# The last down-projection block in seven products, with its operands formed while the block before it is multiplied

## The chip, the cores and the metric

One core of a Trainium2 chip runs the whole kernel as one program. The metric is the device time of one launch in microseconds (us). The engines are TensorE (PE), VectorE (DVE), ScalarE (ACT), GpSimd (POOL) and SyncE (SP), which issues the DMAs. Each has its own instruction queue, worked through in order; they meet only at semaphores. An instruction that waits holds up all that stands behind it on its engine.

## What is computed

Two residual layers run over 768 tokens (512 and 256) of width 1024: a token mixer (mLSTM in layer 0, gated linear attention in layer 1), then a SwiGLU channel mixer. The change touches the channel mixer alone:

```python
D_FF = 2816
def _swiglu(h, w_gu, w_down):
    g, u = jnp.split(h @ w_gu, 2, axis=-1)
    return (jax.nn.silu(g) * u) @ w_down
# in each layer:
h = _rmsnorm(x, norm_ffn_g[i])
x = x + _swiglu(h, ffn_w_gu[i], ffn_w_down[i])
```

## The kernel before

**Splitting into two parts.** Every float32 operand `v` is held as a rounded high part `hi` and the rest `lo = v - hi`. ScalarE writes the high part (a CAST), VectorE the low part (a subtraction). A product is then three matmuls of 128x128 weights on 384 tokens: hi·hi, hi·lo, lo·hi. Tokens are worked on in two halves of 384 (`HT`), and activations lie transposed, channels on partitions.

**Tiles and blocks.** Weights come in tiles of 256 output columns. The 2816 inner channels are eleven groups of 256; group 0 is block 0, groups 2b-1 and 2b are block b, for b = 1 to 5. A "gate" or "up" tile multiplies the 1024 channels of h (eight chunks of 128) into one group. A "down" tile (b, m) multiplies the four chunks of block b into output columns 256m to 256m+255, and adds them to the residual `xT`.

**Seven products.** Plainly, a tile is four groups (two column halves by two token halves); a down tile so done is 4 x 4 chunks x 3 = 48 matmuls (`tile_seq`). The function `fast_tile` does it instead by Winograd's form of Strassen's scheme: a 2x2 block product in seven block products, not eight. A fast down tile is 7 x 2 x 3 = 42 matmuls, a fast gate or up tile 7 x 4 x 3 = 84. For that, sums of blocks are needed on both sides:

- of the weights, four a tile (`fast_sums` and the fourth in `fast_low`): into `s_tmp0`, `s_tmp1` and in place into `raw`. They run on VectorE. The fast tile then has seven weight units, j = 0 to 6, and `fast_high` (ScalarE) and `fast_low` (VectorE) split each in two.
- of the activations, four a block, `T1` to `T4`, besides the plain blocks `B11`, `B21`, `B22`. For h they are made once a layer. For a down block they are made from `sg` and `at` (the silu(gate)·up results of the two groups) while the gate tile after the block runs (`opens`, `middle`), and are stored in `ax0` to `ax5` and `y_parts`.

**Buffers and order.** A weight unit j of the next tile may be split only when product j of the tile at work is done, so while TensorE does tile t, ScalarE and VectorE do the units of tile t+1 between the copies and adds that take tile t out of PSUM. In ScalarE's `fast_work` a tile's four copies out of PSUM (`p1`, `u1`, `p5`, `u2`) stand between the splits; the split of unit 2 waits for the third weight sum, and `p5` stands behind it. Product 5 of a tile waits for the copy `p5` of the same tile. The table `FT` (`fast_order`) sets the order of tiles: gate and up of groups 1 and 2; then for b = 1 to 4 gate and up of group 2b+1, the four down tiles of block b, gate and up of group 2b+2. SyncE loads each tile's weights about two tiles ahead (`load_w`).

**Block 5** is not in `FT`. Its four down tiles follow as plain tiles (`PLAST`): ScalarE and VectorE split whole tiles (`split`, 128x1024), and `last_pair_parts` and `last_parts` split the activations. Under these tiles ScalarE squares each new residual (`squares`), and GpSimd adds the squares into `sq_sum`, one 128x384 add after the other. In layer 0 TensorE needs that sum of the first token half after the third group of the last tile (`first_sum`) for the next norm; in layer 1 right after the last tile (`token_sums`), for the final norm.

## Time and profile before

| what | us |
|---|---|
| median of 3 runs | 1755.4 (1754.39 to 1755.97) |
| the profiled execution | 1752.71 |
| its span, first to last instruction | 1750.9 |
| TensorE busy (matmuls) | 1711.0, 98% |
| VectorE busy | 1164.7, 67% |
| ScalarE busy | 833.5, 48% |
| GpSimd busy | 229.7, 13% |
| mean granted TensorE clock, of full speed | 0.997 |

A line of a timeline gives the start of an instruction (or of a run of like ones, xN) in us from the span's start, its length, the engine, the line of the kernel, the operation with the tile written, the tiles read and the shape, and in brackets the engine's idle time before it with what ended it. Nearly all matmuls have one line, 482, since a helper issues them: they are told apart by their operands. An operation's length is longer than the step to the next one where two overlap in the engine's pipeline; steps are read from starts. The part of the profile that answers the change is the channel mixer's, 376 to 882 us in layer 0 and 1232 to 1738 us in layer 1.

### The profile page before, as it was taken

Reading aid. Unit: us, or ns where it says so; the run is one execution under the profiler, and the core shown is the slowest. Engines: PE = TensorE matmul, PEld = TensorE weight load, DVE = VectorE, ACT = ScalarE, POOL = GpSimd, SP = SyncE. Lnnn points to the kernel's source line nnn. Section 1 sums busy time; section 2 is a strip of 40 time slices with the busy share of each in tenths; the row PEclk is TensorE's granted clock in tenths of the full one; section 3 lists DMA queues with packets and bytes.
Section 4 is the critical chain, followed back from the end, with each engine's and each line's share of the span. In section 5 each row is a group of like instructions: output and inputs, shape, how many; then the busy total and the mean of one; then the engine's idle time right before and its main releaser. Section 6 shows DMA issues by size and latency. Waiting matters only on the chain.

```text
span 1750.9 us, 26390 instructions
## 1 busy us (share of the span) xinstructions
PE 1711.0 (98%) x10042; PEld 1668.6 (95%) x10042; DVE 1164.7 (67%) x2122; ACT 833.5 (48%) x1574; POOL 229.7 (13%) x253
## 2 busy tenths in 40 slices
PE   7999999999999999999999999999999999999998
PEld 6999888999999999999989999999999999999988
DVE  6142455458789898988461366632888888888865
ACT  5222455234455555555442346741445555555543
POOL 4000021360000000000230014425200000000003
PEclk9999999999999999999999999999999999999999
DMA  5320001501313131312232100041031222212121
GB/s 171 121 73 25 25 25 49 166 18 61 97 37 109 37 103 43 98 48 80 82 121 73 49 25 25 25 168 49 19 103 61 65 81 62 84 61 85 61 72 73
DMA packets 108940, 123.75 MB, mean 71 GB/s; under 512 B 4720, under 2 KB 105136, under 8 KB 108560
## 3 DMA queue, kind: packets, MB, share of 16 engines
q1 hardware_dynamic: 107760, 122.00, 21.3%
q8 instruction: 81, 1.33, 0.3%
q14 instruction: 43, 0.35, 0.1%
q10 hardware_dynamic: 1056, 0.07, 0.0%
HBM read 112.62 MB, written 9.44 MB: 70 GB/s over the span
## 4 chain that ended last, share of the span: by engine, by line
PE 80%; DVE 14%; ACT 2%; issue 2%; DMA 1%; POOL 0%; SPq 0%; DVEq 0%; ACTq 0%; POOLq 0%
PE bank L482 79%; DVE xT L1773 4%; DVE w_lo L1731 3%; DVE raw L1715 1%; DVE s_tmp L1718 1%; DVE qkv L1932 1%; DVE s_tmp L1712 1%; DVE w_lo L1689 1%; DVE xT L1950 1%; ACT w_hi L1116 1%; DMA raw<-in_mlstm_w_out_dram 0%; ACT u_five L1214 0%; DVE raw L1736 0%; DVE w_lo L1695 0%; DMA xs<-in_x_prompt_dram 0%
## 5 line engine op out<-in xcount | busy, mean ns | idle before, releaser
L482 PE MATMUL bank<-y_parts,w_hi 128*128 128x384 f32 x1920 | 497.6, 340 | 11.5 <-DVE w_lo L1689 10.4
L482 PE MATMUL bank<-h_hi,w_hi 128*128 128x384 f32 x1280 | 438.6, 343 | 4.5 <-DVE w_lo L1695 1.8
L482 PE MATMUL bank<-h_lo,w_hi 128*128 128x384 f32 x1280 | 432.2, 338 | 0.0
L482 PE MATMUL bank<-h_hi,w_lo 128*128 128x384 f32 x1280 | 431.9, 337 | 0.0
L482 PEld LDWEIGHTS bank<-y_parts,w_hi 128*128 128x128 f32 x1920 | 349.0, 189 | 15.9 <-DVE w_lo L1689 11.6
L482 PE MATMUL bank<-y_parts,w_lo 128*128 128x384 f32 x960 | 324.6, 338 | 0.0
L1158 ACT CAST w_hi<-raw 128x512 fp32r<-128x512 f32 (+1 forms) x360 | 188.9, 526 | 137.9 <-PE bank L482 137.6
L482 PEld LDWEIGHTS bank<-h_hi,w_hi 128*128 128x128 f32 x1280 | 240.6, 188 | 14.5 <-POOL h_lo L2480 3.5
L1731 DVE TENSOR_TENSOR w_lo<-raw,w_hi 128x512 fp32r<-128x512 f32 (+1 forms) x360 | 200.9, 567 | 63.0 <-ACT w_hi L1158 62.0
L482 PEld LDWEIGHTS bank<-h_lo,w_hi 128*128 128x128 f32 x1280 | 240.7, 188 | 1.2 <-issue 0.2
L482 PEld LDWEIGHTS bank<-h_hi,w_lo 128*128 128x128 f32 x1280 | 240.6, 188 | 0.6
L482 PEld LDWEIGHTS bank<-y_parts,w_lo 128*128 128x128 f32 x960 | 181.5, 189 | 0.0
L1689 DVE TENSOR_TENSOR w_lo<-raw,w_hi 128x2048 fp32r<-128x2048 f32 (+2 forms) x40 | 73.0, 1826 | 116.4 <-ACT w_hi L1116 116.2
L482 PE MATMUL bank<-ax,w_hi 128*128 128x384 f32 x512 | 131.4, 338 | 1.1
L1950 DVE TENSOR_TENSOR xT<-xT,bank 128x384 f32<-128x384 f32 x96 | 52.9, 551 | 86.1 <-PE bank L482 82.3
L482 PE MATMUL bank<-w_hi,h_lo 128*128 128x256 f32 x384 | 107.3, 279 | 0.0
L482 PE MATMUL bank<-w_lo,h_hi 128*128 128x256 f32 x384 | 107.3, 279 | 0.0
L482 PE MATMUL bank<-w_hi,h_hi 128*128 128x256 f32 x384 | 107.2, 279 | 0.0
L1116 ACT CAST w_hi<-raw 128x2048 fp32r<-128x2048 f32 (+2 forms) x43 | 64.7, 1506 | 74.8 <-PE bank L482 61.8
L2504 POOL TENSOR_TENSOR sq_sum<-sq_sum,sg 128x384 f32<-128x384 f32 x26 | 27.5, 1058 | 520.8 <-ACT sg L1316 516.7
L482 PEld LDWEIGHTS bank<-ax,w_hi 128*128 128x128 f32 x512 | 92.1, 188 | 3.7 <-ACT u_five L1214 3.7
L1731 DVE TENSOR_TENSOR w_lo<-s_tmp,w_hi 128x512 fp32r<-128x512 f32 (+1 forms) x144 | 81.6, 567 | 7.6 <-ACT w_hi L1158 7.3
(264 smaller groups left out, 2660.7 us busy)
## 6 DMA issues: line engine op xcount, KB each, us to landing
raw<-in_ffn_w_gu_dram SPq DMA_DIRECT2D x44, 1024.0 KB, 5.1
raw<-in_ffn_w_down_dram SPq DMA_DIRECT2D x40, 512.0 KB, 3.5
raw<-in_gla_w_in_dram SPq DMA_DIRECT2D x12, 1024.0 KB, 5.4
raw<-in_mlstm_w_in_dram SPq DMA_DIRECT2D x11, 1024.0 KB, 5.3
x_keep<-xT SPq DMA_DIRECT2D x2, 3072.0 KB, 10.7
xT<-x_keep SPq DMA_DIRECT2D x8, 768.0 KB, 6.6
raw<-in_mlstm_w_out_dram SPq DMA_DIRECT2D x4, 1024.0 KB, 7.1
raw<-in_gla_w_out_dram SPq DMA_DIRECT2D x4, 1024.0 KB, 6.2
```

The source lines that it names most:

```text
L482: return nc.tensor.matmul(out, lhsT, rhs, start=start, stop=stop, skip_group_check=chained)
L1116: nc.scalar.copy(w_hi[s][:, 0:nb, :], raw[s][:, 0:nb, :]).then_inc(w_hi_ready, 1)
L1158: nc.scalar.copy(unit(w_hi, j, nk), w_source(s, j, nk)).then_inc(op_hi if j < 6 else w_hi_ready, 1)
L1689: V.tensor_tensor(w_lo[s][:, 0:nb, :], raw[s][:, 0:nb, :], w_hi[s][:, 0:nb, :].bitcast(F32), ALU.subtract).then_inc(w_lo_ready, 1)
L1712: V.tensor_tensor(s_tmp0[:, 0:nk, :], w_block(s, 0, 0, nk), w_block(s, 1, 0, nk), ALU.subtract).then_inc(op_sum, 1)
L1715: V.tensor_tensor(w_block(s, 1, 0, nk), w_block(s, 1, 0, nk), w_block(s, 1, 1, nk), ALU.add).then_inc(op_sum, 1)
L1718: V.tensor_tensor(s_tmp1[:, 0:nk, :], w_block(s, 1, 0, nk), w_block(s, 0, 0, nk), ALU.subtract).then_inc(op_sum, 1)
L1731: V.tensor_tensor(unit(w_lo, j, nk), w_source(s, j, nk), unit(w_hi, j, nk).bitcast(F32), ALU.subtract).then_inc(op_lo if j < 6 else w_lo_r ...
L1773: return V.tensor_tensor(out, out, src, ALU.add)
L1932: V.scalar_tensor_tensor(out=h_chunk(c, half), in0=xT[:, c, halves[half]], scalar=gain[e][:, c:c + 1], in1=rstd[:, half, :], op0=ALU.mult, ...
L1950: V.tensor_tensor(x, x, src, ALU.add).then_inc(taken[s], 1)
L2504: G.tensor_tensor(sq_sum[:, g // 2, :], sq_sum[:, g // 2, :], sg[:, n % 4, :], ALU.add).then_inc(sq_acc, 1)
```

## The change

Three of the four plain tiles of block 5 become fast tiles. The order of tiles becomes: as before up to block 3, then gate and up of groups 9 and 10, the four down tiles of block 4, three fast down tiles of block 5, and last one plain tile (column block 3), whose weights no longer go through the slot buffers but are split into `y_parts` (`last_w`).

The eight operands of block 5 (`B12` is an eighth, for the plain tile) are formed during the four down tiles of block 4, two a tile (`LATE`). They are stored where h was (`h_hi`, `h_lo`) and in free rows of `y_parts`. ScalarE and VectorE split them (`late_high`, `late_low`), and GpSimd forms the four sums (`late_sums`). GpSimd also forms the four weight sums of every down tile (`down_sums`), 19 a layer; those of gate and up tiles stay on VectorE. The squares of the residual are moved between the last fast tiles, in pieces.

```diff
 def fast_order():
-    for b in range(1, BLOCKS - 1):
+    for b in range(1, BLOCKS - 2):
         out += [("gate", 2 * b + 1, 0), ("up", 2 * b + 1, 0)] + [("down", b, m) for m in range(4)]
         out += [("gate", 2 * b + 2, 0), ("up", 2 * b + 2, 0)]
+    for i in (GROUPS - 2, GROUPS - 1):
+        out += [("gate", i, 0), ("up", i, 0)]
+    out += [("down", BLOCKS - 2, m) for m in range(4)] + [("down", BLOCKS - 1, m) for m in range(3)]
...
+LATE = ((B11, B12), (T1, B21), (T2, T3), (T4, B22))
...
@@ TensorE, after the fast tiles @@
-                q = q0 + PLAST
-                tile_seq(q, 0, a_of(BLOCKS - 1), 4, (a_last_before(0), None, a_last_before(1), None))
-                tile_seq(q, 1, a_of(BLOCKS - 1), 4)
-                tile_seq(q + 1, 0, a_of(BLOCKS - 1), 4)
...
+                tile_begin(q0 + PLAST + 1, 1)
+                pe.wait_ge(a_ready, 4 + 5 * (L + 1))
+                for g in range(4):
...
@@ ScalarE, fast_work @@
+                if late:
+                    late_high(L, late[0])
                 if t >= 2:
                     act.wait_ge(c_out, 3 * (u - 2) + 3)
                 act.wait_ge(p_done, 6 * u + 3)
                 nc.scalar.copy(u_slot(u, "u1"), a).then_inc(p_copied, 1)
...
+                else:
+                    act.wait_ge(raw_loaded[1], 16 * (q + 1))
+                    for k in range(2):
+                        nc.scalar.copy(last_w[0][:, 2 * k:2 * k + 2, :], raw[1][:, 2 * k:2 * k + 2, :]
...
+                if kind == "down" and i == BLOCKS - 1 and m:
+                    squares(PAIRS * L + PLAST, 2 * L + 2, range(4 * m - 4, 4 * m))
...
@@ VectorE, fast_work @@
-                if more:
+                if more and FT[t + 1][0] != "down":
                     fast_sums(L, t + 1)
...
@@ GpSimd @@
+            def down_sums(L, t):
+                pool.wait_ge(raw_loaded[s], 16 * (q + 1))
+                if u:
+                    pool.wait_ge(op_lo, 6 * u - 1)
+                G.tensor_tensor(s_tmp0[:, 0:nk, :], w_block(s, 0, 0, nk), w_block(s, 1, 0, nk), ALU.subtract
...
+                pool.wait_ge(op_sum, 4 * u + 3)
+                pool.wait_ge(op_lo, 6 * u + 1)
+                G.tensor_tensor(w_block(s, 0, 0, nk), w_block(s, 0, 1, nk), s_tmp1[:, 0:nk, :], ALU.subtract
...
+            def ffn(L):
+                for t, (kind, i, m) in enumerate(FT):
+                    if t + 1 < NF and FT[t + 1][0] == "down":
+                        down_sums(L, t + 1)
+                    if kind == "down" and i == BLOCKS - 2:
+                        late_sums(L, m)
...
+                    if kind == "down" and i == BLOCKS - 1 and m:
+                        squares(PAIRS * L + PLAST, 2 * L + 2, range(4 * m - 4, 4 * m))
+                squares(PAIRS * L + PLAST, 2 * L + 2, range(8, 15))
```

GpSimd's queue, before, between the norm's low parts (`h_lo`) and the first squares of layer 0's end; nothing else stands in the whole channel mixer:

```order
L2480 TENSOR_TENSOR h_lo<-qkv,h_hi 128x384 [waits hi_ready] x8
L2587 MEMSET g_hi 128x1024 [waits p_done]
L2588 MEMSET g_lo 128x1024
L2589 MEMSET w_a2_raw 96x1024
L2504 TENSOR_TENSOR sq_sum<-sq_sum,sg 128x384 [waits group_sq,sq_acc,taken0] x2
```

GpSimd's queue after the change, during the first two down tiles of block 4: four weight sums for the second tile, the first sum of block 5's activations, four weight sums for the third tile, two more activation sums:

```order
L2537 TENSOR_TENSOR s_tmp0<-raw1 128x256 [waits op_lo,raw_loaded1]
L2540 TENSOR_TENSOR raw1<-raw1 128x2x128 [waits op_sum]
L2543 TENSOR_TENSOR s_tmp1<-raw1 128x256 [waits op_sum]
L2547 TENSOR_TENSOR raw1<-raw1,s_tmp1 128x2x128 [waits op_lo,op_sum]
L2557 TENSOR_TENSOR sg<-sg 128x768 [waits a_ready,au_lo]
L2537 TENSOR_TENSOR s_tmp0<-raw0 128x256 [waits op_lo,raw_loaded0]
L2540 TENSOR_TENSOR raw0<-raw0 128x2x128 [waits op_sum]
L2543 TENSOR_TENSOR s_tmp1<-raw0 128x256 [waits op_sum]
L2547 TENSOR_TENSOR raw0<-raw0,s_tmp1 128x2x128 [waits op_lo,op_sum]
L2560 TENSOR_TENSOR sg<-at,sg 128x768 [waits au_lo]
L2562 TENSOR_TENSOR sg<-at,sg 128x768 [waits a_ready]
```

A queue that was empty between the norm and the layer's end now runs through all down tiles, each row waiting for VectorE (`op_lo`, `au_lo`).

GpSimd's queue after the change, at the end of layer 0: the weight sums of the last fast tile and then all thirteen adds of squares:

```order
L2547 TENSOR_TENSOR raw0<-raw0,s_tmp1 128x2x128 [waits op_lo,op_sum]
L2527 TENSOR_TENSOR sq_sum<-sq_sum,sg 128x384 [waits group_sq,sq_acc,taken0] x2
L2527 TENSOR_TENSOR sq_sum<-sq_sum,sg 128x384 [waits sq_acc,group_sq,taken1] x4
L2527 TENSOR_TENSOR sq_sum<-sq_sum,sg 128x384 [waits sq_acc,group_sq,taken0] x4
L2527 TENSOR_TENSOR sq_sum<-sq_sum,sg 128x384 [waits sq_acc,group_sq,taken1] x3
```

The adds themselves are the same and in the same order; what moved is the ScalarE squares that they wait for, of which those of the second tile (x4, `taken1`) now stand behind the copies of the last fast tile:

```order
L1248 COPY u_five<-bank2 128x384 [waits p_done,c_out]
L1260 COPY rstd<-bank0 128x384 [waits p_done]
L1342 ACTIVATE sg<-xT 128x384 [waits taken1]
L1342 ACTIVATE sg<-xT 128x384 [waits sq_acc,taken1] x3
```

There ScalarE does its last two copies out of PSUM for the third block-5 tile first, and then the four squares of the second.

## Rows read from the trace of the kernel before

**Rows 1.** the page: busy time, share and instructions of each engine

```profile
PE 1711.0 (98%) x10042; PEld 1668.6 (95%) x10042; DVE 1164.7 (67%) x2122; ACT 833.5 (48%) x1574; POOL 229.7 (13%) x253
```

**Rows 2.** timeline of TensorE, both layers: start, length, line, operation [idle before]

```profile
846.00 1.01 PE L482 MATMUL bank<-y_parts,w_hi 128*128 128x384 f32 x2 [3.57 <-DVE w_lo L1689]
...
1701.75 0.78 PE L482 MATMUL bank<-y_parts,w_hi 128*128 128x384 f32 x2 [3.58 <-DVE w_lo L1689]
```

**Rows 3.** two-microsecond windows: length, busy time of five engines, granted clock, DMA share

```profile
850.00:852.00 2.00, 2.00 (x8) 2.00 (x7) 0.55 (x1) 0.52 (x1) 0.00 (x0) 0.50 0.89 283
1702.00:1704.00 2.00, 2.00 (x8) 2.00 (x8) 2.00 (x4) 0.00 (x0) 0.00 (x0) 0.51 0.53 160
```

**Rows 4.** timeline of VectorE: residual adds of the first plain tile

```profile
850.37 0.55 DVE L1950 TENSOR_TENSOR xT<-xT,bank 128x384 f32<-128x384 f32 x1 [1.42 <-PE bank L482]
853.34 0.55 DVE L1950 TENSOR_TENSOR xT<-xT,bank 128x384 f32<-128x384 f32 x1 [2.42 <-PE bank L482]
...
1705.90 0.56 DVE L1950 TENSOR_TENSOR xT<-xT,bank 128x384 f32<-128x384 f32 x1 [1.19 <-PE bank L482]
```

**Rows 5.** timeline of TensorE: starts of two down tiles, then the fourth tile

```profile
790.67 0.51 PE L482 MATMUL bank<-ax,w_hi 128*128 128x384 f32 x2
...
797.97 0.51 PE L482 MATMUL bank<-ax,w_hi 128*128 128x384 f32 x2
...
810.32 0.34 PE L482 MATMUL bank<-y_parts,w_lo 128*128 128x384 f32 x1
810.79 0.61 PE L482 MATMUL bank<-ax,w_hi 128*128 128x384 f32 x2
```

**Rows 6.** timeline of ScalarE: in the third and fourth down tile of block four

```profile
799.26 0.48 ACT L1185 COPY u_tmp<-bank 128x384 f32<-128x384 f32 x1 [0.69 <-PE bank L482]
...
802.40 0.48 ACT L1214 COPY u_five<-bank 128x384 f32<-128x384 f32 x1 [0.26 <-PE bank L482]
...
809.74 0.62 ACT L1158 CAST w_hi<-s_tmp 128x512 fp32r<-128x512 f32 x1 [0.60 <-DVE s_tmp L1718]
810.27 0.47 ACT L1214 COPY u_five<-bank 128x384 f32<-128x384 f32 x1
```

**Rows 7.** timeline of VectorE: third down tile of block four

```profile
800.00 0.42 DVE L1712 TENSOR_TENSOR s_tmp<-raw 128x256 f32<-128x256 f32 x1
...
802.84 0.55 DVE L1773 TENSOR_TENSOR xT<-xT,bank 128x384 f32<-128x384 f32 x1
803.32 0.42 DVE L1731 TENSOR_TENSOR w_lo<-s_tmp,w_hi 128x256 fp32r<-128x256 f32 x1
803.65 0.42 DVE L1731 TENSOR_TENSOR w_lo<-raw,w_hi 128x256 fp32r<-128x256 f32 x1
```

**Rows 8.** groups of VectorE by form: busy, mean ns, idle before

```profile
L1749 DVE TENSOR_TENSOR ax<-sg,ax 128x768 fp32r<-128x768 f32 x16 | 15.2, 951 | 0.0
```

**Rows 9.** timelines of GpSimd and VectorE, one window each

```profile
344.45 2.74 POOL L2473 TENSOR_TENSOR sq_new<-xT 128x384 f32<-128x384 f32 x1
...
344.21 2.29 DVE L1689 TENSOR_TENSOR w_lo<-raw,w_hi 128x2048 fp32r<-128x2048 f32 x1
...
375.07 10.05 POOL L2480 TENSOR_TENSOR h_lo<-qkv,h_hi 128x384 fp32r<-128x384 f32 x8 [1.04 <-ACT h_hi L1140]
...
377.18 4.78 DVE L1932 SCALAR_TENSOR_TENSOR qkv<-xT,vec,rstd 128x384 f32<-128x384 f32 x4
...
1048.85 1.82 POOL L2546 TENSOR_TENSOR qe<-qe,qkv 128x768 f32<-128x768 f32 x1 [11.00 <-ACT qe L1439]
```

**Rows 10.** timelines of TensorE, GpSimd and ScalarE at the two layer ends

```profile
872.47 1.02 POOL L2504 TENSOR_TENSOR sq_sum<-sq_sum,sg 128x384 f32<-128x384 f32 x1 [0.17 <-POOL sq_sum L2504]
...
881.42 0.88 PE L482 MATMUL bank<-sq_sum,ones 128*128 128x384 f32 x2 [0.88 <-POOL sq_sum L2504]
...
881.70 1.28 ACT L1289 ACT_TABLE_LOAD   x1
...
1737.87 0.58 PE L482 MATMUL bank<-ones,sq_sum 128*128 128x1 f32 x4 [0.60 <-POOL sq_sum L2504]
```

More of the change, by code:

```diff
@@ L1177, in fast_work @@
                 x, y = sg, at
-                middle = kind == "up" and i % 2 == 0 and more
+                middle = kind == "up" and i % 2 == 0 and i < GROUPS - 1
                 opens = kind == "gate" and i % 2 == 1 and i > 1
+                late = LATE[m] if kind == "down" and i == BLOCKS - 2 else None
                 n_sum = 4 * (NA * L + i // 2 - 1)
@@ L1707, in fast_sums @@
                 q, s = PAIRS * L + PFAST + t // 2, t % 2
-                nk = 2 if kind == "down" else 4
+                nk = 4
                 dve.wait_ge(raw_loaded[s], 16 * (q + 1))
@@ L1763, in fast_work @@
                 own = pair_of[i % 2]
-                middle = kind == "up" and i % 2 == 0 and more
+                middle = kind == "up" and i % 2 == 0 and i < GROUPS - 1
                 opens = kind == "gate" and i % 2 == 1 and i > 1
+                late = LATE[m] if kind == "down" and i == BLOCKS - 2 else None
                 n_unit = 7 * (NA * L + i // 2 - 1)
@@ L2489, in y_low, with squares @@
                 low(Y_S[L] + 4 * h + g, y_lo[c][:, hs], y_hi[c][:, hs])
-            def squares(q, e):
-                for n in range(15):
+            def squares(q, e, steps=range(15)):
+                for n in steps:
                     i, s, g = n // 8, n // 4 % 2, n % 4
```

200 lines of the change are left out of this document (116 added, 84 removed).

## The prediction, written before the changed kernel was run

> **What bounds the kernel now.** I read the page first: TensorE is busy for 1711.0 of 1750.9 us [rows 1], so what is gained or lost is matmuls, their pace, or TensorE's idle time. Then TensorE's timeline, to see where it idles in the channel mixer. One hole stands out in each layer: 3.57 and 3.58 us ahead of the first plain tile of block 5, ended by VectorE's low part of the weights [rows 2]. A whole tile's weights can be split only when the last fast tile is through with the slot, and then ScalarE and VectorE work one after the other with TensorE idle. The windows behind the hole show the granted clock at 0.50 and 0.51 [rows 3], its lower level (1.2 GHz): TensorE had been idle for those 3.6 us. Last, the fourth down tile of a block: 0.47 us between two matmuls that otherwise start 0.17 apart, and a first pair of 0.61 us in place of 0.51 [rows 5]. ScalarE shows why: its split of unit 2 waited for VectorE's third weight sum, and the copy `p5`, which product 5 needs, stood behind it [rows 6]. That is 0.4 us, once in each of four blocks and two layers.
>
> **What goes, step by step.** (1) Products. A down tile of 42 matmuls takes 797.97 - 790.67 = 7.30 us, 0.174 us each [rows 5]. Three tiles a layer lose 6 matmuls each: 2 x 18 x 0.174 = 6.3 us. (2) The hole. After the last up tile now comes a fast tile, with its weights split unit by unit; such a change from up to down occurs in blocks 1 to 4 with no hole. 3.57 + 3.58 = 7.15 us. The last plain tile's weights go to rows of their own and are split early, so I expect no new hole of this kind. (3) The slow clock. Group 0 of the first plain tile is 12 matmuls, 2.09 us at full pace, and its residual add starts about 0.28 us behind its end. The add came 4.37 us after the start in layer 0 and 4.15 in layer 1, where 2.37 is due; group 1 in layer 0 took 2.97 in place of 2.09 [rows 2, 4]. Lost: 2.0 + 0.9 + 1.8 = 4.7 us, which go with the hole. (4) The small holes at the ends of blocks. With four weight sums a down tile gone from VectorE (0.42 us each [rows 7]) it reaches the gate tile's sums over a microsecond sooner; the wait was 0.4 us. 8 x 0.4 = 3.2 us. Sum: 6.3 + 7.15 + 4.7 + 3.2 = 21.3 us.
>
> **What comes: VectorE under block 4.** Its steps are 0.34 us for a low part of 256 columns and about 0.50 for a residual add [rows 7], so a down tile is 7 x 0.34 + 7 x 0.50 = 5.9 us, well below 7.30. In block 4 two late low parts of 768 columns are added, 0.95 us long and some 0.87 in step [rows 8]: 5.9 + 1.74 = 7.64 a tile. By this alone VectorE falls behind by 0.34 x 4 = 1.3 us.
>
> How far may it fall behind? Not a whole tile. GpSimd's first weight sum for tile t+1 waits for low part 4 of tile t. On time, that low part is done 0.25 us before TensorE starts tile t. GpSimd's adds step at 1.02 + 0.17 us for 384 columns [rows 10]; between that and 1.82 for 768 [rows 9] one of 256 columns is about 0.75 long and steps at 0.92. Three sums end some 2.5 us into the tile (2.2 if nothing is in their way). ScalarE must then split unit 2 (0.33 in step) and copy `p5` (0.48 [rows 6]) before product 5 starts, 5.2 us into the tile: the third sum must be there by 4.4. So the slack is 2.2 us, and everything beyond becomes idle time of TensorE at product 5.
>
> **GpSimd and VectorE get in each other's way.** A GpSimd product of 384 columns lasted 2.74 us [rows 9], where an add of that size takes 1.02 [rows 10]: it had been issued 0.24 us behind a VectorE subtraction of 2.29 us with two SBUF operands, and ended 0.69 us after that one. And where both queues are full, VectorE's operations of 384 columns step at 4.78 / 4 = 1.2 us and GpSimd's at 10.05 / 8 = 1.26 [rows 9]: they take turns. VectorE alone would step at 0.5, so a GpSimd operation of 1.02 us costs it 0.7, its length less 0.3. Adds with an operand in PSUM I take to be left alone, since they read SBUF once. The Trainium skill, "SBUF — State Buffer", section "Who interferes with whom", says the same of the kind: a VectorE instruction with two SBUF inputs contends with a GpSimd one that reads SBUF, and whoever comes second blocks fully. By the section's words it is a rule against this change; the traces agree with it. Had they shown free running, the next sum would be nil.
>
> Per layer GpSimd runs in block 4 sixteen weight sums, 0.75 - 0.3 = 0.45 us each, and four activation sums, 1.82 - 0.3 = 1.5 each: 7.2 + 6.0 = 13.2 us of turns that VectorE can lose. No row prices what part it does lose. Nothing is the lower end; all of it the upper. I walked both queues through the four tiles, each operation waiting for the other's turn: the activation sums cost about 1 us each (4.2; VectorE is then at adds from PSUM for part of it), the weight sums 0.2 each (3.3; three of four start in gaps or under such adds). 7.5 us in all; the row it is nearest to is the one of turns. VectorE is then 1.3 + 7.5 = 8.8 us late at the end of block 4, 6.6 more than the slack. TensorE idles 6.7 us a layer, in two to five holes at product 5, mostly in tiles 3 and 4 of block 4 and the first of block 5. 2 x 6.7 = 13.4 us. In block 5 VectorE's tile is 5.9 + 4 x 0.3 = 7.1 us, so it loses no more. I charge nothing for the clock there: idle times of over 3 us may bring it down, but a slower tile then only fills the next hole.
>
> **What comes: the layer ends.** TensorE needs 14 squares of the residual summed (`first_sum`) at the third group of the last tile. The squares of tile (5,1) now stand on ScalarE behind the copies of tile (5,2), about 5.9 us into it; GpSimd starts on n = 4 at 6.4 and has ten adds to do at 1.19: it ends at 18.3. The group of the last tile ends at 7.3 + 6.26 = 13.6. In layer 0 it waited 0.88 us before [rows 10], and would wait 4.7 now: +3.8, and some 0.8 for two or three adds that meet VectorE's splits, less 0.7 since the table load that stood on the path behind it (881.70, 1.28 us [rows 10]) is done by then: +3.9. In layer 1 the last tile ends at 15.65 and the token sums wait till 18.3, 2.6 us; the wait was 0.60 by the row [rows 10]: +2.0. Sum 5.9 us. Bounds: nothing, if GpSimd is further on than that, and 9, if four more of the ten adds in each layer lose a turn of 0.4. The weights of the last tile are ready by then, unless VectorE is late; that wait would be taken from the same 5.9.
>
> **The sum.** -21.3 + 13.4 + 5.9 = -2.0 us. Against the profiled execution, 1752.7 (its span is 1.8 shorter): 1750.7. The median of the three runs lies 2.7 higher, so 1755.4 - 2.0 = **1753.4**.
>
> **Rivals.** *A: VectorE keeps up.* If sums fall into gaps and under adds from PSUM, TensorE idles 0 to 4 us a layer in place of 6.7. For it: GpSimd's 0.75 us is an estimate, and VectorE has 1.4 us a tile of adds that meet nobody. Against: the turns of [rows 9]. With 1.5 us a layer: 21.3 - 3.0 - 5.9 = 12.4, so 1743. *B: slower.* Every turn is lost: 1.3 + 13.2 - 2.2 = 12.3 us a layer in block 4: 21.3 - 24.6 - 5.9 = -9.2, so 1764.6. The place is again product 5 behind ScalarE's wait for the third sum; the kernel is slower than before from 7.7 us a layer on, (21.3 - 5.9) / 2. Against it: the queues are not both full all the time. *C: the small holes stay,* since three sums on GpSimd take 2.5 us where VectorE needed 1.3 for them, and the split of unit 2 now waits in each down tile of blocks 1 to 3. From 2.2 us of lateness on, each of 24 tiles gives a hole. On time there is 2.2 us of room, so this has little weight; with 0.5 us a tile it is 12 us, so 1765.
>
> **Chances.** Forecast (TensorE idles 4 to 9 us a layer there) 0.45, its own range 1748 to 1758; A 0.3; B 0.15; C 0.05; anything else 0.05. Time 1753.4. A and the upper part of my own case reach down to 1741, B up to 1763: the range is 1741 to 1763. A measurement of this kernel can tell about 0.2%, 3.5 us, from no change. Faster by more takes A and the fourth of my own case with under 6 us a layer: 0.42. Slower by more takes B, C, the rest: 0.25. Within: 0.33.
>
> **What would show it.** 10006 matmuls in place of 10042; no idle row of 3.6 us ahead of block 5, and no window at 0.5 there. In TensorE's timeline, idle rows at product 5 of block 4's tiles ended by ScalarE's copy `p5`, and on ScalarE a wait for GpSimd's sum ahead of it. GpSimd's 256-column sums at 0.75 us where alone, over 1 us where VectorE is at work. VectorE without idle time in block 4. A wait of 4 to 5 us for `sq_sum` in layer 0's end and of 2.6 in layer 1's. The forecast is wrong if block 4 shows under 4 us of idle TensorE a layer (A), or if blocks 1 to 3 show holes in every down tile (C); if the layer ends wait under 1 us, the step on the squares was wrong.

## The result, and the profile after

| | before | after |
|---|---|---|
| median, us | 1754.9 (1753.67 to 1755.97, 4 runs) | 1771.0 (1770.13 to 1771.67, 4 runs) |
| ratio of after to before | | 1.0092, 95% interval 1.0077 to 1.0107 |
| span of the profiled execution | 1750.9 | 1768.4 |

The changed kernel is 16 us slower. 1753.4 had been forecast, with a range of 1741 to 1763: the time lies above all of it. The page of the kernel after, first the line that answers to [rows 1], then the tenths of forty equal slices for TensorE:

```profile
PE 1712.0 (97%) x10006; PEld 1666.1 (94%) x10006; DVE 1211.0 (68%) x2054; ACT 854.8 (48%) x1640; POOL 378.8 (21%) x413
...
PE   7999999999999999998889999999999999999987
```

The 36 matmuls are gone, and TensorE is busy as long as before. VectorE gave up 152 weight sums of 0.42 us [rows 7], some 64 us, and is busy 46 us *longer*, more than its new low parts can explain (experiment 2 has the number). That is the first sign of what went wrong. What TensorE waits for, in the profile's list of waits (total, times, longest):

```profile
PE bank L496 <- POOL sq_sum L2527: 13.7, 2, 7.2
PE bank L496 <- ACT u_five L1248: 12.8, 11, 2.6
...
PE bank L496 <- DVE w_lo L1752: 2.4, 4, 0.7
```

Both holes of [rows 2] are gone. In their place stand TensorE's waits in block 4 and the first tile of block 5, here layer 0's, from TensorE's timeline (start, length, line, operation, idle before with what ended it):

```profile
826.11 0.61 PE L496 MATMUL bank<-ax,w_hi 128*128 128x384 f32 x2 [0.72 <-ACT u_five L1248]
...
832.14 0.59 PE L496 MATMUL bank<-ax,w_hi 128*128 128x384 f32 x2 [0.56 <-DVE w_lo L1752]
...
834.07 0.59 PE L496 MATMUL bank<-y_parts,w_hi 128*128 128x384 f32 x2 [0.65 <-DVE w_lo L1752]
...
838.00 0.62 PE L496 MATMUL bank<-ax,w_hi 128*128 128x384 f32 x2 [2.65 <-ACT u_five L1248]
...
848.26 0.62 PE L496 MATMUL bank<-ax,w_hi 128*128 128x384 f32 x2 [1.09 <-ACT u_five L1248]
...
857.45 0.61 PE L496 MATMUL bank<-y_parts,w_hi 128*128 128x384 f32 x2 [1.62 <-ACT u_five L1248]
...
875.01 4.37 PE L496 MATMUL bank<-h_lo,y_parts 128*128 128x384 f32 x24
```

They add up to 7.3 us. `u_five` is the copy `p5`; two of the six, 1.2 us, were for a low part of VectorE itself. From the first matmul of block 4 (812.70) to the last plain tile (875.01) are 62.3 us; seven tiles of 42 matmuls at 0.174 are 51.1. So 11.2 us are lost. Behind the longest wait the granted clock fell to its lower level (1.2 GHz). Layer 1 loses the same, 1675.60 to 1737.88, 62.3 us. The windows answer to [rows 3], at another place:

```profile
840.00:842.00 2.00, 2.00 (x8) 2.00 (x7) 2.00 (x3) 0.41 (x1) 1.60 (x1) 0.50 0.11 39
1702.00:1704.00 2.00, 2.00 (x8) 2.00 (x8) 1.97 (x4) 0.97 (x3) 1.52 (x1) 0.50 0.60 200
```

That slow clock cost nothing in the end. Here are the seven tiles of layer 0 and of layer 1, and, from the profile of experiment 9, where layer 0 is the same program, layer 0 once more (the last three numbers are granted clock, DMA share and GB/s):

```profile
812.70:875.01 62.31, 54.93 (x295) 52.26 (x295) 61.04 (x101) 37.27 (x90) 34.15 (x33) 0.97 0.20 60
1675.60:1737.88 62.28, 55.80 (x295) 53.13 (x295) 61.01 (x101) 37.36 (x89) 31.44 (x30) 0.95 0.17 52
```

```profile
814.00:876.28 62.28, 53.38 (x295) 50.64 (x295) 61.02 (x101) 37.26 (x90) 34.12 (x33) 1.00 0.20 60
```

The length is 62.3 us each time, with the clock at 0.97, 0.95 and 1.00. Where it stayed at 1.00, TensorE was busy for less and waited for more (the wait that is 1.09 at 848.26 was 2.63 there). VectorE, the third engine in these rows, was busy for 61 of the 62.3 us in all three: it sets the pace.

ScalarE's timeline before the last of these waits shows the way there as forecast: the split of unit 2 waits for GpSimd's third sum, and the copy stands behind it.

```profile
856.62 0.40 ACT L1173 CAST w_hi<-s_tmp 128x256 fp32r<-128x256 f32 x1 [2.29 <-POOL s_tmp L2543]
856.93 0.47 ACT L1248 COPY u_five<-bank 128x384 f32<-128x384 f32 x1
```

**VectorE beside GpSimd.** The second down tile of block 4, first GpSimd's timeline and then VectorE's, same stretch:

```profile
822.15 0.74 POOL L2537 TENSOR_TENSOR s_tmp<-raw 128x256 f32<-128x256 f32 x1 [2.70 <-DVE w_lo L1752]
822.97 0.80 POOL L2540 TENSOR_TENSOR raw<-raw 128x256 f32<-128x256 f32 x1
823.85 1.33 POOL L2543 TENSOR_TENSOR s_tmp<-raw 128x256 f32<-128x256 f32 x1
825.94 0.78 POOL L2547 TENSOR_TENSOR raw<-raw,s_tmp 128x256 f32<-128x256 f32 x1 [0.76 <-DVE w_lo L1752]
827.62 2.10 POOL L2560 TENSOR_TENSOR sg<-at,sg 128x768 f32<-128x768 f32 x1 [0.90 <-DVE h_hi L1773]
829.68 2.03 POOL L2562 TENSOR_TENSOR sg<-at,sg 128x768 f32<-128x768 f32 x1
```

```profile
822.39 0.79 DVE L1752 TENSOR_TENSOR w_lo<-raw,w_hi 128x256 fp32r<-128x256 f32 x1
823.10 1.49 DVE L1773 TENSOR_TENSOR y_parts<-sg,y_parts 128x768 fp32r<-128x768 f32 x1
824.51 0.54 DVE L1804 TENSOR_TENSOR xT<-xT,bank 128x384 f32<-128x384 f32 x1
824.98 1.16 DVE L1752 TENSOR_TENSOR w_lo<-raw,w_hi 128x256 fp32r<-128x256 f32 x3
826.06 1.48 DVE L1773 TENSOR_TENSOR h_hi<-sg,h_hi 128x768 fp32r<-128x768 f32 x1
827.46 0.55 DVE L1804 TENSOR_TENSOR xT<-xT,u_tmp 128x384 f32<-128x384 f32 x1
828.04 0.55 DVE L1804 TENSOR_TENSOR xT<-xT,bank 128x384 f32<-128x384 f32 x1
828.51 1.48 DVE L1752 TENSOR_TENSOR w_lo<-s_tmp,w_hi 128x256 fp32r<-128x256 f32 x1
829.92 2.07 DVE L1752 TENSOR_TENSOR w_lo<-raw,w_hi 128x256 fp32r<-128x256 f32 x1
```

A low part of 256 columns takes 0.42 us alone. The one issued at 828.51 ends at 829.99, behind GpSimd's sum (827.62 + 2.10 = 829.72); the next ends at 831.99, behind the second sum (831.71). Adds with an operand in PSUM (`bank`), in the middle of such a sum, keep their 0.55. Low parts of 768 columns take 1.48 in place of 0.95. And GpSimd's third weight sum, which ran into one of them, took 1.33 in place of 0.8. So the two engines meet outside their semaphores as well. The three low parts from 824.98 on recur at 836.88, 847.12 and 856.33: VectorE's tiles last 11.9, 10.2 and 9.2 us, where 7.64 and some turns had been expected.

**The layer ends**, TensorE's timeline; these answer to [rows 10], where the waits were 0.88 and 0.60 (the pair at 888.63 is a slow one too, 1.62 us in place of 0.88):

```profile
888.63 1.62 PE L496 MATMUL bank<-sq_sum,ones 128*128 128x384 f32 x2 [7.15 <-POOL sq_sum L2527]
...
1753.02 1.41 PE L496 MATMUL bank<-ones,sq_sum 128*128 128x1 f32 x6 [6.58 <-POOL sq_sum L2527]
1754.29 2.80 PE L1119 MATMUL bank<-ident,y_fin 128*128 128x128 f32 x12
```

**Where 17.5 us came from** (span after less span before, from starts in the two traces): GpSimd's first `qe` product in layer 1's token mixer starts at 1008.42 and started at 1001.16, +7.3 for layer 0; the token sums start at 1753.02 and started at 1737.87, another +7.9 for layer 1; and +2.35 stand behind the token sums, of which 2.05 stand between the token sums and the 36 transposes (5.42 us in place of 3.37), at the lower clock.

### The profile page after: what moved, and what is told of

Its sections match the earlier page's. It is cut to its first block, busy times and chain, and to the rows that moved or that the text cites. A ratio compares the mean times of both kernels' runs of the same rounds, so it can differ in the third digit from the quotient of the medians.

```text
span 1768.4 us, 26558 instructions
## 1 busy us (share of the span) xinstructions
PE 1712.0 (97%) x10006; PEld 1666.1 (94%) x10006; DVE 1211.0 (68%) x2054; ACT 854.8 (48%) x1640; POOL 378.8 (21%) x413
## 3 DMA queue, kind: packets, MB, share of 16 engines
q8 instruction: 81, 1.33, 0.3%
## 4 chain that ended last, share of the span: by engine, by line
PE 82%; DVE 12%; issue 2%; ACT 2%; DMA 1%; POOL 0%; SPq 0%; DVEq 0%; ACTq 0%; POOLq 0%
PE bank L496 81%; DVE xT L1804 3%; DVE w_lo L1752 3%; DVE qkv L1960 1%; DVE xT L1978 1%; ACT w_hi L1131 1%; DVE w_lo L1710 1%; DVE h_hi L1773 1%; DMA raw<-in_mlstm_w_out_dram 0%; DVE y_fin L2409 0%; DVE w_lo L1716 0%; PE bank L1119 0%; DMA xs<-in_x_prompt_dram 0%; ACT w_hi L1138 0%; PE bank L618 0%
## 5 line engine op out<-in xcount | busy, mean ns | idle before, releaser
L496 PE MATMUL bank<-h_hi,w_hi 128*128 128x384 f32 x1376 | 463.4, 342 | 4.4 <-DVE w_lo L1716 1.8
L496 PE MATMUL bank<-y_parts,w_hi 128*128 128x384 f32 x1688 | 436.2, 339 | 9.0 <-ACT u_five L1248 3.2
L496 PEld LDWEIGHTS bank<-y_parts,w_hi 128*128 128x128 f32 x1688 | 305.3, 188 | 14.0 <-ACT u_five L1248 5.3
L1752 DVE TENSOR_TENSOR w_lo<-raw,w_hi 128x512 fp32r<-128x512 f32 (+1 forms) x390 | 247.0, 647 | 82.6 <-ACT w_hi L1173 80.7
L496 PE MATMUL bank<-y_parts,w_lo 128*128 128x384 f32 x844 | 284.7, 337 | 0.0
L2537 POOL TENSOR_TENSOR s_tmp<-raw 128x256 f32<-128x256 f32 x38 | 28.2, 741 | 761.0 <-DVE w_lo L1752 761.0
L496 PEld LDWEIGHTS bank<-y_parts,w_lo 128*128 128x128 f32 x844 | 158.9, 188 | 0.0
L1710 DVE TENSOR_TENSOR w_lo<-raw,w_hi 128x2048 fp32r<-128x2048 f32 (+1 forms) x32 | 62.6, 1957 | 110.4 <-ACT w_hi L1131 110.3
L1752 DVE TENSOR_TENSOR w_lo<-s_tmp,w_hi 128x512 fp32r<-128x512 f32 (+1 forms) x156 | 94.7, 607 | 11.8 <-ACT w_hi L1173 11.5
L1173 ACT CAST w_hi<-s_tmp 128x512 fp32r<-128x512 f32 (+1 forms) x156 | 81.1, 520 | 37.5 <-POOL s_tmp L2543 21.6
L1131 ACT CAST w_hi<-raw 128x2048 fp32r<-128x2048 f32 (+1 forms) x35 | 56.4, 1612 | 72.8 <-PE bank L496 62.7
## 6 DMA issues: line engine op xcount, KB each, us to landing
x_keep<-xT SPq DMA_DIRECT2D x2, 3072.0 KB, 10.7
```

The costliest lines, as they stand in the source:

```text
L496: return nc.tensor.matmul(out, lhsT, rhs, start=start, stop=stop, skip_group_check=chained)
L1131: nc.scalar.copy(w_hi[s][:, 0:nb, :], raw[s][:, 0:nb, :]).then_inc(w_hi_ready, 1)
L1173: nc.scalar.copy(unit(w_hi, j, nk), w_source(s, j, nk)).then_inc(op_hi if j < 6 else w_hi_ready, 1)
L1710: V.tensor_tensor(w_lo[s][:, 0:nb, :], raw[s][:, 0:nb, :], w_hi[s][:, 0:nb, :].bitcast(F32), ALU.subtract).then_inc(w_lo_ready, 1)
L1752: V.tensor_tensor(unit(w_lo, j, nk), w_source(s, j, nk), unit(w_hi, j, nk).bitcast(F32), ALU.subtract).then_inc(op_lo if j < 6 else w_lo_r ...
L2537: G.tensor_tensor(s_tmp0[:, 0:nk, :], w_block(s, 0, 0, nk), w_block(s, 1, 0, nk), ALU.subtract).then_inc(op_sum, 1)
```

## Experiments

The ratio is always against the kernel before on the same chip, with its 95% interval.

**1. Who gains from GpSimd's sums: all of them back on VectorE.**

```diff
-                nk = 4
+                nk = 2 if kind == "down" else 4
-                if more and FT[t + 1][0] != "down":
+                if more:
                     fast_sums(L, t + 1)
...
-                    if kind == "down" and i == BLOCKS - 2:
-                        late_sums(L, m)
```

> The changed kernel with all of GpSimd's new sums back on VectorE: the four weight sums of every down tile and the four activation sums of block 4. GpSimd then does nothing in the down tiles. Theory 1 (turns: VectorE loses to each GpSimd sum about what doing the sum itself would cost): by the steps of the kernel before a VectorE tile in block 4 is 5.9 + 1.74 + 4 x 0.42 + about 1.0 = 10.3 us against the 10.5 it took in the changed kernel (starts of its 768-column low parts 11.9, 10.2 and 9.3 us apart), so the time stays near the changed kernel's: 1766 to 1773. Theory 2 (the sums on GpSimd cost more than they save): TensorE idles less in block 4, and the time is 1755 to 1765. Theory 3 (GpSimd does relieve VectorE, the late low parts are too much alone): slower than the changed kernel, over 1775.

Measured: 1770.9 us, ratio 1.0088 (1.0073 to 1.0103), the same as the changed kernel. Theory 1. TensorE's waits for `u_five` are 18.0 us in place of 12.8 + 2.4 for `w_lo`, and the layer-end waits 13.8. The small holes at block ends are 0.15 us again. So 160 sums moved off VectorE bought it nothing.

**2. The same waits on GpSimd and no shorter lengths (1.05 us for a weight sum of 0.8), but nothing read.**

```diff
-                G.tensor_tensor(s_tmp0[:, 0:nk, :], w_block(s, 0, 0, nk), w_block(s, 1, 0, nk), ALU.subtract
-                                ).then_inc(op_sum, 1)
+                fill(s_tmp0[:, 0:nk, :]).then_inc(op_sum, 1)
... (all eight kinds of sum alike; fill is three memsets in a row)
```

> The changed kernel with each new GpSimd sum replaced by three fills of the same output with ones, one after the other: the same waits and releases, about the same length on GpSimd (1.0 us for 256 columns, 2.4 for 768), but nothing is read from SBUF. The sums themselves are left out, so the output is not the reference's. Theory 1 (turns at SBUF reading): VectorE's low parts in block 4 are back at 0.34 and 0.95 us, its tile is 7.64 us, TensorE idles under 2 us a layer there, the small holes at the ends of blocks 1 to 3 go, the layer ends are less late: 1747 to 1754. Theory 2 (the chain of three sums on GpSimd is too long by itself, whatever it reads): the holes at product 5 stay, 1765 or more. Theory 3 (VectorE is overloaded by the late low parts alone): tile periods stay over 9 us, 1762 or more.

Measured: 1750.9 us, ratio 0.9972 (0.9961 to 0.9984): 20 us faster than with the sums, inside theory 1's 1747 to 1754. VectorE's timeline in the same tile:

```profile
830.99 1.09 DVE L1752 TENSOR_TENSOR w_lo<-raw,w_hi 128x256 fp32r<-128x256 f32 x3
832.00 0.95 DVE L1773 TENSOR_TENSOR h_hi<-sg,h_hi 128x768 fp32r<-128x768 f32 x1
832.87 0.55 DVE L1804 TENSOR_TENSOR xT<-xT,u_tmp 128x384 f32<-128x384 f32 x1
```

All at their length alone. VectorE is busy 1153.1 us in this run, with the same 2054 instructions that took 1211.0 in the changed kernel: 58 us are turns lost, about as much as the 64 us moved. And the tile (825.19 to 832.87, from one `u_tmp` add to the next) is 7.68 us; 7.64 had been worked out. TensorE waits 1.3 us in block 4. The small holes at the ends of blocks 1 to 3 are gone as well. Theories 2 and 3 fall: neither the chain of three sums nor the late low parts alone is the cost, but what GpSimd reads.

**3. The two kinds of sums apart.** First fills for the activation sums alone, then fills for the weight sums alone (the same edits as in 2, in one of the two functions).

> The changed kernel with only the four activation sums of block 4 (768 columns) as three fills each on GpSimd, so that they read nothing; the weight sums are real and read SBUF as before. The activation sums are left out, so the output is not the reference's. All fills together gave 1750.9 against the changed kernel's 1771.0: 20.1 us. Theory 1 (the long activation sums are what the turns in block 4 cost, weight sums cost 0.2 us each as the prediction walked them): most of the 18.6 us of block 4 comes back, the small holes at block ends stay, 1754 to 1758. Theory 2 (the sixteen weight sums a layer cost their full turn, 0.45 us or more each): 1761 to 1766.

> The opposite: the weight sums of all down tiles as three fills each, the activation sums real. The weight sums are left out, so the output is not the reference's. Theory 1 (activation sums are the cost): the small holes at the ends of blocks 1 to 3 go (3.2 us) and little else, 1763 to 1768. Theory 2 (weight sums cost the more): 1754 to 1759. If the two parts add up, this gain and the one with the activation sums filled together make 20.1 us; if TensorE's slack of 2.2 us hides the first part of either, they make more.

Measured: 1762.8 us (ratio 1.0051, 1.0036 to 1.0066) and 1761.1 (1.0030, 1.0019 to 1.0041). With the activation sums gone 8 us come back, with the weight sums gone 10, together 18 of the 20. The first lies in theory 2's range; the second lies between the two theories. So both kinds cost. The weight sums look like the larger part, but the two intervals overlap. With the activation sums alone real, each turn shows by itself; GpSimd's timeline, then VectorE's:

```profile
818.44 2.10 POOL L2563 TENSOR_TENSOR sg<-sg 128x768 f32<-128x768 f32 x1 [0.80 <-DVE h_lo L1773]
...
827.55 1.84 POOL L2566 TENSOR_TENSOR sg<-at,sg 128x768 f32<-128x768 f32 x1
829.36 2.03 POOL L2568 TENSOR_TENSOR sg<-at,sg 128x768 f32<-128x768 f32 x1
```

```profile
819.33 1.49 DVE L1752 TENSOR_TENSOR w_lo<-s_tmp,w_hi 128x256 fp32r<-128x256 f32 x1
...
828.08 1.60 DVE L1752 TENSOR_TENSOR w_lo<-s_tmp,w_hi 128x256 fp32r<-128x256 f32 x1
829.60 2.07 DVE L1752 TENSOR_TENSOR w_lo<-raw,w_hi 128x256 fp32r<-128x256 f32 x1
```

With the one of the fourth sum, 1.59 us, that is 1.07 + 1.18 + 1.65 + 1.17 = 5.1 us lost a layer. Lengths over 0.42, 0.55 and 0.95 in the other run, with the weight sums alone real, add up to 6.1 us beside the four sets of weight sums of layer 0 (VectorE, 813 to 847 us).

**4. Only the activation sums back on VectorE.**

> The changed kernel with only the four activation sums of block 4 (768 columns) back on VectorE; the weight sums stay on GpSimd. In the traces so far VectorE's low parts that began during such a GpSimd sum lasted 1.49, 1.60 + 2.07 and 1.59 us in place of 0.42: 5.1 us a layer for four sums, while VectorE's own step for one is about 0.87. Theory 1 (a low part waits for the end of the GpSimd sum, so moving a sum there saves nothing): VectorE is 5.1 - 4 x 0.87 = 1.6 us a layer less late, 1771 - 3.2 = 1768. Theory 2 (GpSimd's sums do relieve VectorE, in net): slower than the changed kernel, 1774 or more.

Measured: 1769.1 us, ratio 1.0081 (1.0065 to 1.0096). The direction is theory 1's; the gain is 1.9 us where 3.2 was worked out, and the two intervals overlap, so it is no more than a hint. Theory 2, that GpSimd relieves VectorE, falls.

**5. The hole alone, in the kernel before.** The first plain tile's weights and the operands of group 9 are split under the last up tile, and that tile's groups 0 and 1 are multiplied side by side:

```diff
+                else:
+                    act.wait_ge(raw_loaded[0], 16 * (q + 2))
+                    for k in range(2):
+                        nc.scalar.copy(last_w[0][:, 2 * k:2 * k + 2, :], raw[0][:, 2 * k:2 * k + 2, :]
+                                       ).then_inc(last_hi if k == 0 else w_hi_ready, 1)
...
-                tile_seq(q, 0, a_of(BLOCKS - 1), 4, (a_last_before(0), None, a_last_before(1), None))
+                tile_begin(q, 0)
+                for last in side_by_side([of_last(0), of_last(1)], a_of(BLOCKS - 1), 0, 4, a_last_before(0)):
+                    last.then_inc(mm_done[0], 1)
...
```

> The kernel before, block 5 still in four plain tiles, GpSimd as before; only the hole ahead of them is closed: the first plain tile's weights are split into rows 2 and 3 of y_parts during the last up tile, where VectorE and ScalarE have no next fast tile to prepare, the operands of group 9 are split there too, and the first plain tile's groups 0 and 1 run side by side so that its last activation operand is wanted 18 matmuls into the tile. Theory 1 (hole and slow clock are one cost and both go): 3.57 + 3.58 us of idle TensorE and 4.7 us of slow matmuls behind it, 1754.9 - 11.8 = 1743, and no window at 0.5 after 846 and 1702 us. Theory 2 (a new wait of 1 to 2 us for the last activation operand takes its place): 1746 to 1750. Theory 3 (the slow clock falls there whatever the hole): 1748, with windows still at 0.5.

Measured: 1743.1 us, ratio 0.9930 (0.9914 to 0.9945): 12.2 us faster than before, where 11.8 was expected (the expectation took the waits of 3.57 and 3.58 us; by starts the hole is 3.91 us in place of 0.17, which makes up the rest). **This version beats both kernels.** TensorE's timeline over the place of the hole, and a window behind it:

```profile
843.79 0.34 PE L483 MATMUL bank<-h_hi,w_lo 128*128 128x384 f32 x1
843.97 7.30 PE L483 MATMUL bank<-y_parts 128*128 128x384 f32 x41
```

```profile
846.00:848.00 2.00, 2.00 (x14) 2.00 (x13) 1.42 (x2) 1.62 (x2) 0.00 (x0) 1.00 0.00 0
```

Forty-one matmuls without a wait, 14 in two microseconds in place of 8, the clock at 1.00.

**6. The order at a block's end, in that version.** ScalarE's copy `p5` ahead of its split of unit 2:

```diff
+                turn = kind == "down" and m == 3
-                if more:
+                if more and not turn:
                     fast_high(L, t + 1, 2)
...
                 nc.scalar.copy(u_slot(u, "p5"), bank[4 * s + 2][:, 0:HT]).then_inc(p_copied, 1)
+                if turn:
+                    fast_high(L, t + 1, 2)
```

> The kernel before with its hole closed as in the run of 1743.1 us, and at the fourth down tile of each block ScalarE's copy p5 put ahead of its split of unit 2, which waits for VectorE's third sum. Theory 1 (product 5 waits only since its copy stands behind that split): the small holes of 0.31 us and the first pair of 0.61 in place of 0.51 go, 8 x 0.4 = 3.2 us: 1740. Theory 2 (VectorE is late there anyway, and the next waiter, product 6 or 7 of the same tile or the next tile's product 3, waits as long): 1743.

Measured: 1742.2 us, ratio 0.9931 (0.9916 to 0.9946), no difference that can be told from 1743.1. ScalarE's timeline shows why little is to be had:

```profile
545.96 0.48 ACT L1235 COPY u_five<-bank 128x384 f32<-128x384 f32 x1 [0.56 <-PE bank L483]
546.33 0.63 ACT L1169 CAST w_hi<-s_tmp 128x512 fp32r<-128x512 f32 x1
546.86 0.62 ACT L1169 CAST w_hi<-raw 128x512 fp32r<-128x512 f32 x1
547.38 0.48 ACT L1249 COPY rstd<-bank 128x384 f32<-128x384 f32 x1
```

`p5` is in time now, but the copy of unit 2's product (`rstd`) has two splits of 512 columns ahead of it. Behind it a gap of about 0.1 us and a first pair of 0.62 us are left one product later. Theory 2's kind, in smaller measure.

**7. The layer end: ScalarE's squares sooner.** The four squares of tile (5,1) ahead of the copies of the last tile's weights, instead of at the end of tile (5,2).

> The changed kernel with the four squares of tile (5,1) on ScalarE ahead of the copies of the last tile's weights instead of at the end of tile (5,2). Theory 1 (GpSimd's chain of ten adds sets the layer end): GpSimd starts some 2 us sooner on it, the wait for sq_sum of 7.15 and 6.5 us falls by 1.5 to 2 in each layer, 1771.0 - 3.5 = 1767.5. Theory 2 (the residual itself is late, since VectorE is): ScalarE's squares of (5,2) wait for VectorE's adds all the same, and the copies p5 and u2 behind the squares stop TensorE at product 5 of (5,2): within 1.5 us of 1771 or slower.

Measured: 1774.5 us, ratio 1.0111 (1.0095 to 1.0126), 3.5 us slower by the medians, though the intervals overlap. Both halves of the theories came true: the waits for `sq_sum` fell from 13.7 to 10.7 us, and the copies behind the squares stopped TensorE 2.38 us in each layer at product 5 of tile (5,2). In block 4 of layer 0 the waits are 0.73, 0.55, 0.65, 2.64, 2.64 and 1.61, 1.5 us more than in the changed kernel, but the slow stretch behind the fourth, some 1.6 us, is not there; why the clock held is open. The seven tiles last 64.7 us, 2.4 more than in the changed kernel: the stop at product 5, and nothing else. At the program's end the low clock lasted longer: from the token sums to the end of the last transpose 12.2 us in place of 9.5 (1753.02 to 1762.57), a stretch that differs from profile to profile (experiment 9). With 4.8 lost at product 5 and 3.0 won at `sq_sum` that makes 4.5, where the medians differ by 3.5.

**8. The layer end: four of GpSimd's adds made short.**

```diff
+                        nc_ = 16 if 4 <= n < 8 else HT
-                        G.tensor_tensor(sq_sum[:, g // 2, :], sq_sum[:, g // 2, :], sg[:, n % 4, :], ALU.add
+                        G.tensor_tensor(sq_sum[:, g // 2, 0:nc_], sq_sum[:, g // 2, 0:nc_], sg[:, n % 4, 0:nc_], ALU.add
```

> The changed kernel, all its sums real, but GpSimd's adds of the squares n = 4 to 7 in block 5 take in 16 of 384 columns: four of the ten adds ahead of first_sum are nearly free, each still waited for as before. The rest of those squares is left out, so the output is not the reference's. Theory 1 (as predicted: GpSimd's chain of adds from n = 4 on sets the layer end): the waits of 7.15 and 6.5 us fall by 4 x 1.19 less what n = 8 then has to wait, 4 us a layer: 1763. Theory 2 (n = 8 is ready only when VectorE, late from block 4, has added tile (5,2) into the residual): GpSimd then waits for ScalarE's square instead, and what is left is only what its own adds took from VectorE in that tile, up to 2 us a layer: 1767 to 1771.

Measured: 1766.7 us, ratio 1.0069 (1.0054 to 1.0084), 4.3 less than the changed kernel, 2.1 a layer (the intervals just overlap; in the profile the two waits are 4.2 us shorter). This is theory 2's edge, not the 4 us a layer of theory 1. The waits were 4.99 and 4.51 us. GpSimd, early now, waited 1.54 us for the square n = 8, whose residual comes from VectorE. What was won is VectorE's: its three adds of tile (5,2) with both operands in SBUF took 0.57, 0.57 and 0.56 us in place of 1.38, 1.37 and 1.19.

**9. The layer end: VectorE's order in layer 1.** The adds of the last tile's groups 0 and 1 ahead of the scalings of `y_fin`.

```diff
-                    for half in range(2):
-                        for c in range(6):
-                            scaled(c, half)
-                    for g in range(4):
-                        add_residual(q, 1, g, 6 + g % 2)
+                    for half in range(2):
+                        for g in (2 * half, 2 * half + 1):
+                            add_residual(q, 1, g, 6 + g % 2)
+                        for c in range(6):
+                            scaled(c, half)
...
-                pe.wait_ge(fin_scaled, 12 + t // 3 * 2 + 2 if hf else 12)
+                pe.wait_ge(fin_scaled, 8 * (t // 3) + (8 if hf else 6))
```

> The changed kernel with another order of VectorE's last operations in layer 1: the residual adds of groups 0 and 1 of the last tile ahead of the twelve scalings of y_fin, and six of these behind them, then groups 2 and 3; TensorE's transposes wait for eight and sixteen scalings accordingly. In the changed kernel GpSimd's add of n = 12 waited 3.01 us for a square whose residual add stood behind 7.30 us of scalings. Theory 1 (in layer 1 it is VectorE's order, not the length of GpSimd's chain, that the last wait of 6.58 us ends with): the wait falls by about 3 us, 1768. Theory 2 (GpSimd's chain of adds is as late anyway, as the prediction had it): within 1 us of 1771.

Measured: 1771.5 us, ratio 1.0092 (1.0078 to 1.0106). The wait did fall by what theory 1 said, from 6.58 to 3.51 us, but the median did not. TensorE's timeline:

```profile
1751.32 0.80 PE L496 MATMUL bank<-ones,sq_sum 128*128 128x1 f32 x6 [3.51 <-POOL sq_sum L2528]
...
1757.76 6.43 PE L1119 MATMUL bank<-ident,y_fin 128*128 128x128 f32 x36
```

In the changed kernel the same 36 transposes took 4.13 us, started at 1758.44, and ended at 1762.57; here they end at 1764.19, in a trace that was 1.4 us later at GpSimd's add n = 4 already (its clock had also been low from 301.6 to 305.0 us, which the kernel after's was not). The window from 1756 to 1762 has a granted clock of 0.50; the kernel after had 1.00 from 1758 on. In this pair of profiles the gain was given back in the slow clock. That the shorter wait is the reason is not shown: behind waits as long as the changed kernel's, 6.58 or 6.59 us, the same 36 transposes took 4.13 us in the changed kernel, 5.55 in experiment 4, 6.98 in the first run of experiment 3 and 7.09 in experiment 1, so that the end of the program, from the token sums on, took 9.5, 11.8, 13.3 and 13.4 us. This spread is as large as the gain that was looked for. What is shown is that the wait ended with VectorE's order; what its 3 us are worth in time stays open. The same order in the best version (with the edit of 6):

> The kernel before with its hole closed and p5 ahead of the split at block ends (1742.2 us), and the residual adds of the last tile's groups 0 and 1 ahead of the scalings in layer 1. Theory 1 (the token sums' wait of 0.6 us in layer 1 ends with VectorE's order): 1741.5. Theory 2 (VectorE, not late here, now idles for groups 0 and 1 with its scalings undone, and the transposes of the second half wait for them): 1743 to 1744.

Measured: 1742.8 us, ratio 0.9930 (0.9917 to 0.9942); it can't be told from either of the two others.

**10. The layer end without any reading by GpSimd.** The kernel of experiment 2, and the adds n = 4 to 14 as fills too:

```diff
+                        if n >= 4:
+                            fill(sq_sum[:, g // 2, :], 2).then_inc(sq_acc, 1)
+                            continue
```

> The run with all new sums as fills (1750.9 us), and GpSimd's adds of the squares n = 4 to 14 in block 5 as two fills each of 384 columns, some 1.1 us a step as an add takes when it is alone. Neither sums nor squares are added, so the output is not the reference's. No GpSimd instruction that reads SBUF is left in block 5 beside VectorE from n = 4 on. Theory 1 (the layer end is late by the length of the chain of ten steps, as the prediction had it, and by what the adds lose to VectorE): the chain from n = 4 to 13 lasts 11 to 12 us in place of 14.2, the twelve scalings of y_fin last 4.8 us in place of 9.1, the waits of 6.75 and 5.36 us fall to about 4.5 and 3: 1750.9 - 4.6 = 1746. Theory 2 (the chain is late by its length alone): within 1 us of 1750.9.

Measured: 1743.2 us, ratio 0.9934 (0.9917 to 0.9951), 7.7 us less than with the adds. The chain from n = 4 to 13 takes 10.6 us in place of 14.2 in layer 0, and the waits are 3.11 and 2.79 us in place of 6.75 and 5.36. The fills stepped at 1.04 us, a little shorter than an add's 1.19: ten steps, 1.5 us, of the 3.6 that the chain lost, are length and not turns. Theory 2 falls. Theory 1 holds in kind and was too low in size, 7.7 us where 4.6 was worked out: layer 0's wait fell further than to 4.5. And it was wrong on VectorE's scalings, which took nearly as long as beside the adds:

```profile
1715.11 7.03 DVE L2409 TENSOR_SCALAR y_fin<-xT,vec 128x384 f32<-128x384 f32 x12
```

In the kernel before, with a single GpSimd add beside them, the same twelve took 4.84 us (one of them 1.21, the others 0.41 or 0.42), and beside the adds 7.30 (kernel after) and 9.10 (experiment 2).

## Why the prediction was wrong, point by point

| step (both layers, us) | forecast | measured |
|---|---|---|
| products | -6.3 | 36 matmuls fewer, taken at -6.3 |
| hole | -7.15 | gone, -7.5 by starts |
| slow clock behind it | -4.7 | gone, -4.7 (with the hole 12.2 in experiment 5) |
| small holes at block ends | -3.2 | -1.1 |
| TensorE in block 4 | +13.4 | +22.3 |
| layer ends | +5.9 | +12.2 |
| slow clock behind the last wait | 0 | +2.05 |
| sum | -2.0 | +17.0 (spans: +17.5) |

Of the 0.5 us between the last two, 0.35 were there before the change could act: layer 0's channel mixer starts at 376.87, and started at 376.52.

**The gains** (1) to (3) were right, in place and size; the hole and its clock alone are worth 12.2 us where 11.85 stood in the sum.

**The small holes** (4) were mostly kept. At five of the six ends of blocks 1 to 3 TensorE's idle time fell from 0.11 to 0.15 us to 0.04 to 0.06, at the sixth (1497.45) it grew to 0.40; some 0.3 us in all. Block 4's two, 0.8 us, are gone because no gate tile follows there now. The step took four weight sums off VectorE and forgot the turns, although these were charged in block 4: in block 3 three weight sums met low parts, and the fourth met the add from `u_tmp`, which has both operands in SBUF and took 1.09 us in place of 0.55 (706.10). In experiment 2, and in the run of experiment 3 with fills for the weight sums alone, they went.

**VectorE under block 4** is the step that failed. Its own work was right: 7.64 us a tile worked out, 7.68 seen once GpSimd read nothing. The mechanism was right too, and for most of the waits the place (product 5, behind the split of unit 2). What was mis-sized is the turns, 7.5 us a layer. In the kernel after, VectorE's lengths over 0.42, 0.55 and 0.95 between 812 and 850 us add up to 10.8.

- Weight sums were walked at 0.2 us each, 3.3, since "three of four start in gaps or under such adds". They cost 5.9. Three of the four start beside low parts (0.37, 0.54 and 0.53 us lost in the tile shown above, and 0.07 at 824.98). GpSimd's first and fourth sum are released by a low part of VectorE, which is at its next low part 0.1 to 0.3 us later.
- Activation sums were put at 1 us each, 4.2. They cost 4.8 there, and 5.1 in experiment 3.

Together that is 3.3 of the 4.5 us that each layer lost beyond the forecast. Most of the rest is the slack, put at 2.2 us. Even in the third down tile of block 3, where VectorE is nearly on time, GpSimd's first sum starts 0.6 us into the tile (710.52, the tile at 709.92), not 0.25 before it, and the third ends 3.1 us into it, not 2.5; it must be there by 4.4, so the slack was 1.3. The forecast's own sum with these sizes, 1.3 late + 10.8 of turns - 1.3 of slack, is 10.8, an estimate, and the pair of matmuls behind each of the six waits is 0.1 later still; 11.2 was measured. The clock in block 4 was charged at nothing since "a slower tile then only fills the next hole". That was right: 62.3 us at any of the three clocks above.

**The rule cited** from the Trainium skill ("SBUF — State Buffer", section "Who interferes with whom") holds to the word in this trace: a low part issued 0.9 us into a GpSimd sum ended 0.3 us behind it, adds from PSUM kept 0.55 us, and fills left VectorE's low parts alone. In the prediction it had been called a rule against the change. Rival B, every turn lost, gave 12.3 us a layer in block 4 and 1764.6; 11.2 came there, so B was closer than the forecast, and 0.15 was too small a chance for it. Its time was still 6 us too low, since it used the same layer ends and kept the gain of the small holes.

**The layer ends** were the second failure, 12.2 for 5.9. In layer 0 the wait was put at 4.7 and 0.8 for turns; it was 7.15, as the chain from n = 4 to 13 took 14.6 us and not 11.9. Of that, two adds of 1.77 beside VectorE's splits, one of 1.51, and 0.75 us for a square whose residual VectorE brought late. "Less 0.7", for the table load, came true and was lost again: the load (887.50 to 888.78) was done 1.5 us before ScalarE needed it, but the pair behind the wait took 1.62 us in place of 0.88 at the lower clock. In layer 1 the step named the wrong end of the wait. It priced GpSimd's chain; GpSimd in fact stood 3.01 us, waiting for a residual add behind 7.30 us of VectorE's scalings, which the sum never looked at; with those adds ahead of the scalings the wait was 3.51 (experiment 9). Behind the wait the program's last matmuls ran at the lower clock, 2.05 us in this profile and more in others of the same wait.

**Rivals A and C.** A (VectorE keeps up) is what experiment 2 shows, with the turns taken away. C asked for a hole in every down tile of blocks 1 to 3; none is there, and VectorE catches up in each block.

## What to carry to other kernels

Moving an elementwise operation from VectorE to GpSimd frees VectorE only as far as no VectorE instruction with two SBUF operands (or a scaling from SBUF to SBUF) lies beside it. In this kernel 160 sums moved gave nothing. So count the move at nothing, not at its length, until the trace shows which VectorE instructions it will lie beside. An operation that is released by an instruction of VectorE starts as VectorE goes on to its next one; here three of four weight sums met a low part that way or behind it. A slow clock behind a wait costs nothing where another engine sets the pace. Where a hole stands in front of a tile, first try to take out the hole alone: here it was worth 12 us, and going on from there to the 6 us of saved products left the kernel 28 us slower than that.
